# Two expert tables gathered apart in rows of 4 KB, the second by four tokens' 32 picks, on one Trainium2 core

## What is computed

```python
def block(args):
    xt, it, gt = args                     # tokens, 128 picks, 128 gates
    act = jax.nn.gelu(jnp.einsum('td,tkd->tk', xt, peer_u[it]), approximate=False)
    return jnp.einsum('tk,tkd->td', gt * act, peer_v[it])
```

## Time and profile before

| | us |
|---|---|
| median of three runs | 2607.96 |
| the runs | 2607.25 to 2612.75 |
| span of the profiled execution | 2607.3 |
| PE busy | 2152.8 |
| DVE busy | 1647.3 |
| ACT busy | 1003.4 |
| POOL busy | 702.4 |

### The profile page before, as it was taken

One profiled execution on the slowest core, in us unless ns is written; L12 is line 12 of the kernel. 1 busy time (PEld: TensorE's weight loads), 2 busy tenths in 40 slices (PEclk: granted clock), 3 DMA queues, 4 the chain that ended last, 5 costly groups with the idle time before them and its releaser, 6 DMA issues. The chain is left out here.

```text
span 2607.3 us, 25567 instructions
## 1 busy us (share of the span) xinstructions
PE 2152.8 (83%) x8090; PEld 1334.7 (51%) x8090; DVE 1647.3 (63%) x3381; ACT 1003.4 (38%) x2477; POOL 702.4 (27%) x610
## 2 busy tenths in 40 slices
PE   6999978897878687877868887676777787899998
PEld 6778855676423232322324453232333474788877
DVE  5674266535888988878456776656766555555534
ACT  3213345323443343333334344435533455433322
POOL 0120031000444354443434454444444100000000
PEclk8999988998999899898989999787988897999999
DMA  7664200211899999999999999999999433222222
GB/s 243 218 208 113 67 5 26 77 61 75 340 419 420 400 403 420 396 420 398 415 380 415 414 414 411 420 370 359 420 419 420 159 92 122 91 97 97 80 81 97
DMA packets 142827, 683.18 MB, mean 262 GB/s; under 512 B 19648, under 2 KB 36320, under 8 KB 74224
## 3 DMA queue, kind: packets, MB, share of 16 engines
q0 software_dynamic: 73728, 536.90, 50.3%
q1 hardware_dynamic: 68976, 144.78, 17.0%
HBM read 679.50 MB, written 2.10 MB: 261 GB/s over the span
## 5 line engine op out<-in xcount | busy, mean ns | idle before, releaser
L2483 PE MATMUL peer_Y<-peer_w,peer_diag 128*128 128x512 f32 x1784 | 902.5, 645 | 242.2 <-ACT peer_diag L2469 215.2
L2428 POOL DMA_INDIRECT peer_w<-in_peer_uv,peer_eidx x510 | 606.4, 1189 | 703.7 <-PE peer_Y L2483 465.8
L2437 DVE CUSTOM_DVE_ANT_0 peer_w<-peer_w,peer_xtok 128x1024 f32<-128x1024 f32 x510 | 617.7, 1222 | 198.1 <-DMA peer_w<-in_peer_uv,peer_eidx 195.3
L2483 PEld LDWEIGHTS peer_Y<-peer_w,peer_diag 128*128 128x128 f32 x1784 | 337.8, 202 | 753.2 <-ACT peer_diag L2469 443.7
L2461 ACT ACTIVATE peer_gel<-peer_dots 128x1 f32<-128x1 f32 x512 | 103.8, 203 | 721.8 <-DVE peer_dots L2437 721.5
L2469 ACT ACTIVATE peer_diag<-all_ident,peer_a 128x128 f32<-128x128 f32 x448 | 179.8, 401 | 18.1 <-PE peer_Y L2483 3.6
L2463 ACT ACTIVATE peer_a<-peer_gel,peer_gates 128x1 f32<-128x1 f32 x512 | 150.8, 294 | 16.6
L2992 PE MATMUL m_acc<-m2x_hs,m2x_cut 128*128 128x512 f32 (+1 forms) x384 | 143.7, 374 | 6.4 <-PEq L123 3.7
L2993 PE MATMUL m_acc<-m2x_hs,m2x_cut 128*128 128x512 f32 (+1 forms) x384 | 143.3, 373 | 0.0
L2994 PE MATMUL m_acc<-m2x_hs,m2x_cut 128*128 128x512 f32 (+1 forms) x384 | 143.2, 373 | 0.0
L1293 ACT ACTIVATE p_cut<-m1h_raw 128x512 fp32r<-128x512 f32 (+2 forms) x96 | 58.2, 609 | 202.1 <-PE p_acc L1240 119.3
(11 more groups left out here) (518 smaller groups left out, 3731.2 us busy)
## 6 DMA issues: line engine op xcount, KB each, us to landing
m_gates<-in_w_ada SPq DMA_DIRECT2D x48, 512.0 KB, 4.3
m2x_raw<-in_w_up SPq DMA_DIRECT2D x22, 1024.0 KB, 4.8
m1h_raw<-in_w_in SPq DMA_DIRECT2D x80, 256.0 KB, 3.1
m20h_raw<-in_w_in SPq DMA_DIRECT2D x48, 256.0 KB, 7.3
m22h_raw<-in_w_in SPq DMA_DIRECT2D x48, 256.0 KB, 2.8
m_down_ring<-in_w_down SPq DMA_DIRECT2D x22, 512.0 KB, 3.4
m_out_ring<-in_w_out SPq DMA_DIRECT2D x16, 512.0 KB, 7.8
peer_w<-in_peer_uv,peer_eidx POOLq DMA_INDIRECT x510, 16.7
```

The source lines that it names most:

```text
L2428: pool.indirect_dma_start(self.slot(n).rearrange("p c n -> p (c n)"), None, self.uv_dram, bass.IndirectOffsetOnAxis(self.col(self.eidx, n) ...
L2437: dve.tensor_tensor_reduce(u, u, self.xtok[:, n // PICKS, :], 1.0, 0.0, ALU.mult, ALU.add, self.col(self.dots, n)).then_inc(self.dotted, 1)
L2483: ins = pe.matmul(self.Y[:, h, :], self.diag[:, i % self.RD, :], self.slot(n)[:, 1, h * BANK:(h + 1) * BANK], start=(k == 0), stop=(i == l ...
```

## The change

- The two tables stay apart in memory. One indirect DMA fetches 128 rows of 4 KB from one of them: 512 DMAs for `u`, 512 for `v`. The ring has 16 slots of 512 KB and 4 lent ones.
- The order of the fetches is `u` 0 to 31 alone, then `u` s and `v` s - 32 in turn, then the last 32 of `v` alone. A step of the gather now ends 33 steps after its `u`: `STANDALONE` is 289, `STEPS` 545.
- A `u` fetch takes one pick of 128 tokens, as before. A `v` fetch takes 32 picks of four tokens: partition 32i + r holds pick r of token 4b + i of the tile. For this, tokens are dealt to partitions (token 4b + i at partition 32i + b): by 16 more DMAs from `xtok` to `xrow` in `norm_rows`, issued on SP behind the early loads, SP waiting for them, and by a permuted copy of the queries into `qT`. The picks and the weights are transposed in blocks of 32 x 32 by DVE: `eidxT` (one more piece in each top-k call), `aT`.
- ACT makes gelu for 32 picks at once, DVE the gated weights, ACT places them in `Z`, which holds for each of 32 fetches 128 x 32 stationary values, zero outside of the token's own picks. DVE clears `Z` once ahead of the first step.
- PE sums over the 128 partitions of a `v` fetch: output of 32 tokens, on column strip q of the array for fetches 8q + m. Four fetches make a batch, eight matmuls of 32 stationary columns and 512 moving ones, and the batch frees its four slots at its end. There are no diagonals, and none of the picks is folded on DVE.
- DVE takes two pieces of the top-k a step in the first 32 steps, three up to step 112, then two.

The core of the diff:

```diff
-    RW, RD = 9, 4
-    LOW, FIRST = 2, 4
-    FOLDED = range(2 * PICKS, NT * PICKS)
-    SHARE = 4
+    RW = 16
+    LOW, FIRST = 4, 8
+    GROUP = 32
+    GROUPS = NT * PICKS // GROUP
+    BATCH = 4
...
+        for s in range(self.N + self.GROUP):
+            if s < self.N:
+                self.order.append(("u", s))
+            if s >= self.GROUP:
+                self.order.append(("v", s - self.GROUP))
...
+    def consumed(self, item):
+
+        kind, n = item
+        return (self.dotted, n + 1) if kind == "u" else (self.used, n // self.BATCH + 1)
...
     def fetch(self, pool, limit):
         for n in range(self.fetched, limit):
+            kind, i = self.order[n]
             if n == self.FIRST:
                 pool.wait_ge(*self.vacated)
-            if n % (2 * TOPK) == 0:
-                pool.wait_ge(self.picked, TopK.picked_at(n))
+            if i % self.GROUP == 0:
+                pool.wait_ge(self.picked if kind == "u" else self.idx_turned, TopK.picked_at(i))
             if n >= self.RW + len(self.lent):
-                pool.wait_ge(*self.consumed(n - self.RW))
-            pool.indirect_dma_start(self.slot(n).rearrange("p c n -> p (c n)"), None, self.uv_dram,
-                                    bass.IndirectOffsetOnAxis(self.col(self.eidx, n), 0)).then_inc(self.landing(n)[0], 16)
+                pool.wait_ge(*self.consumed(self.order[n - self.RW]))
+            t, k = divmod(i, PICKS)
+            if kind == "u":
+                table, idx = self.u_dram, self.eidx[:, t, k:k + 1]
+            else:
+                b = self.token_row(i)
+                table, idx = self.v_dram, self.eidxT[:, t, k // self.GROUP * self.GROUP + b:k // self.GROUP * self.GROUP + b + 1]
+            pool.indirect_dma_start(self.slot((kind, i)), None, table, bass.IndirectOffsetOnAxis(idx, 0)).then_inc(self.landing((kind, i))[0], 16)
...
+        if s < self.N:
+            dve.wait_ge(*self.landing(("u", s)))
+            u = self.slot(("u", s))
+            dots = self.dots[:, s // self.GROUP % 2, s % self.GROUP:s % self.GROUP + 1]
+            dve.tensor_tensor_reduce(u, u, self.xrow[:, s // PICKS, :], 1.0, 0.0, ALU.mult, ALU.add, dots).then_inc(self.dotted, 1)
...
+            dve.tensor_tensor(self.a[:], self.gel[:], self.gates[:, t, k:k + self.GROUP], ALU.mult).then_inc(self.weighed, 1)
+            dve.wait_ge(self.weighed, g + 1)
+            if g >= 1:
+                dve.wait_ge(self.placed, 4 * g)
+            dve.transpose(self.aT[:], self.a[:]).then_inc(self.turned, 1)
...
+            for i in range(4):
+                rows = slice(32 * i, 32 * i + 32)
+                dst = self.Z[rows, g % 2, :].rearrange("p (q x) -> p q x", q=4)[:, :, i:i + 253:36]
+                act.activation(dst, self.aT[rows, :].rearrange("p (q r) -> p q r", q=4), ACT.Copy).then_inc(self.placed, 1)
...
+        for item in items:
+            pe.wait_ge(*self.landing(item))
         for h in range(2):
-            ins = pe.matmul(self.Y[:, h, :], self.diag[:, i % self.RD, :], self.slot(n)[:, 1, h * BANK:(h + 1) * BANK],
-                            start=(k == 0), stop=(i == last))
+            for q, item in enumerate(items):
+                b = self.token_row(item[1])
+                ins = pe.matmul(self.Y[32 * q:32 * q + 32, h, :], self.Z[:, g % 2, 32 * b:32 * b + 32], self.slot(item)[:, h * BANK:(h + 1) * BANK],
+                                start=(first % PICKS == 0), stop=(first % PICKS == PICKS - self.BATCH))
         ins.then_inc(self.used, 1)
...
-    FAST, PACES = 112, (3, 2)
-    done_by = lambda s: PACES[0] * min(s + 1, FAST) + PACES[1] * max(0, s + 1 - FAST)
+    SLOW, FAST = 32, 112
+    done_by = lambda s: 2 * (s + 1) + max(0, min(s + 1, FAST) - SLOW)
...
+            dve.memset(gather.Z[:], 0.0).then_inc(gather.zeroed, 1)
...
             load_early(sp, early_landed, early)
+            if dealt is not None:
+                for t in range(NT):
+                    sp.wait_ge(scaled, t + 1)
+                    for i in range(4):
+                        sp.dma_start(dealt[32 * i:32 * i + 32, t, :], xn[i:P:4, t, :]).then_inc(dealt_out, 16)
+                sp.wait_ge(dealt_out, 16 * 4 * NT)
...
+            dve.wait_ge(self.picked, call + 1)
+            dve.transpose(self.eidxT[:, t, ks], self.eidx[:, t, ks]).then_inc(self.turned, 1)
```

More of the change, by code:

```diff
@@ L2278, in vector @@
         hs, ks = slice(h0, h0 + n), slice(h0 * K, (h0 + n) * K)
-        stage = max(j for j in range(22) if self.start(call, j) <= i)
+        stage = max(j for j in range(23) if self.start(call, j) <= i)
         j = i - self.start(call, stage)
@@ L2452, in vector @@
+        t, at = divmod(s - self.GROUP, PICKS)
+        if at == 0 and t >= 1:
+            dve.wait_ge(self.used, t * PICKS // self.BATCH)
             for h in range(2):
@@ L2471, in tensor @@
     def tensor(self, pe, s):
-        n = s - 1
-        if not 0 <= n < self.N or not self.on_pe(n):
+        first = s - self.GROUP - self.BATCH + 1
+        if first < 0 or first % self.BATCH or first >= self.N:
             return
-        t, k = divmod(n, PICKS)
-        i = self.products(n)
-        pe.wait_ge(self.diaged, i + 1)
-        pe.wait_ge(*self.landing(n))
-        if k == 0 and t >= 1:
+        g, m = divmod(first // self.BATCH, self.GROUP // self.BATCH)
+        t = first // PICKS
@@ L2485, in tensor, with pick @@
         ins.then_inc(self.used, 1)
-def pick(nc, gather, top, qT, keys, mod, rows, steps):
-    ident = gather.consts["ident"]
-    FAST, PACES = 112, (3, 2)
-    done_by = lambda s: PACES[0] * min(s + 1, FAST) + PACES[1] * max(0, s + 1 - FAST)
+def pick(nc, gather, ident, top, qT, keys, mod, rows, steps):
+    SLOW, FAST = 32, 112
+    done_by = lambda s: 2 * (s + 1) + max(0, min(s + 1, FAST) - SLOW)
     calls = range(1, len(TopK.CALLS))
@@ L2557, in _ @@
         def _(pool):
-            gather.fetch_to(pool, gather.STEPS + 3)
+            gather.fetch_to(pool, gather.STEPS)
         @block.vector
```

144 lines of the change are left out of this document (71 added, 73 removed).

## The result

The changed kernel takes 2835.9 us, the median of four runs (2830.3 to 2845.6), where the kernel before took 2607.6 beside it (2606.8 to 2612.8). The ratio is 1.0878, with a 95% interval of 1.0854 to 1.0902: slower by 228 us, against 180 forecast. Where a text says first or second measurement, it means these two.

What follows compares the result with a forecast made beforehand. Transfers bounded the gather before; POOL's issues were to bound it after the change. The span of 2607.3 us plus 10 for dealing x and 170 for the longer gather gave 2787, forecast as 2788 us, range 2635 to 2890.

Steps and rivals of the forecast that it cites:

- Bound and sign: In the gather, POOL replaces the DMA engines as bound: 2.98 us per pair against 2.5 of transfer; slower, chance 0.92.
- An issue costs by rows: On POOL, an indirect DMA with its pause stays at 1.49 us for 128 rows, though the rows shrink to 4 KB.
- The price of a collision: On POOL, a dot product blocks an issue's start with chance 0.86, costing 0.53 us in the mean, 0.46 per dot.
- rival 2: In the gather, fixed dot timing hits each pair, or strips in turn make POOL wait for slots: 2935 us; chance 0.10.
- POOL waits for nothing: In the gather, POOL issues without waits for slots; its other work in the stretch adds only 11 us.
- The first 32 steps: At the gather's start, DVE paces steps at 2.0 us, 64 us in all; 44 issues begun by 734.4; memset 1.1.
- The deal of x: Before the query opens, SP's 16 uncovered DMAs take 7.0 us of issues and 2 to 3 to land: +10 us.
- Tail: Behind the gather's last issue, landing 3.4, last batch on PE 4 and two additions 1.3: +9 us.
- Behind the gather: After the last addition of Y, the remaining 571 us are untouched by the change.
- The four strips: On PE, a batch takes 8.1 us in turn, a quarter together; neither bounds; slot reuse needs 11.5 of 13.4 us.
- Rival 1: In the gather, transfers stay the bound: 2606 to 2665 us, 2640 at its middle; chance 0.22 for 2613 to 2700.
- Rival 3: In the gather, twenty half slots fill the transfer holes: 2566 us; chance 0.08 together with the lower edge of Rival 1.

Runs made afterwards that it cites:

- second measurement: The changed kernel, unchanged, measured again beside later experiments: 2785.4 us, ratio 1.0676.
- half rows: The changed kernel with rows of 2 KB, the fetched half of each used twice, so as many issues and half the bytes: 2857.8 us.
- first measurement: The changed kernel, unchanged, as first measured against the kernel before: 2835.9 us, ratio 1.0878.
- one-operand kernels: The changed kernel with dot products replaced by sums of the fetched row alone: 2691.9 us; with three norms' roots also made reciprocals on VectorE: 2655.2 us.

## Why the prediction came out as it did

The direction, the mechanism and nearly the size were right: 2788 forecast, 2836 and 2785 measured. That the second lies 3 us from the forecast is luck: two terms of the sum are off by over 60 us each, in opposite directions. Its steps one by one.

*Bound and sign.* POOL takes the place of the transfers. Right: the rate fell to 354 to 375 GB/s, POOL's waits for slots from 466 to 48 us, and halving the bytes gained nothing. POOL's busy time in the stretch was to be about 1230 us; it is 1171 (1024 x 1.134 and 10 of roots).

*An issue costs by rows.* Right, and the choice that carries the forecast: 1.13 us for rows of 4 KB where 1.19 had been taken over from 8 KB; undisturbed 0.95 for both, and for 2 KB no less. One of the supports of 1.49 was misread: from the issue at 669.06 to that at 680.79 there are seven steps and not eight, 1.68 us each and not 1.47, so this stretch did not agree with the mean. The sum rests on the mean alone.

*The price of a collision.* Mis-sized. I took a chance of 0.86 at 0.53 us, 0.46 for a dot. In the second measurement 475 of 512 dots are met by a start, 0.93, but such an issue takes 1.26, only 0.31 over 0.95. Starts are not spread evenly over a dot but locked to it, a fixed time behind the landing; rival 2 had named that as a risk, and here the phase falls kindly. With half rows it falls badly, 0.48. An issue with its pause came to 1.42, not 1.49: 980 x 0.07 = 69 us less than the sum has (1.43 in the first measurement, 59 less).

*POOL waits for nothing.* The step that failed. I gave POOL's other work +11 and found no wait in its way; in the second measurement the pauses over 0.35 us are 73 in all, in the first 108. I had looked for who is held up when DMAs are moved past a queue, but only on SP; the roots on POOL itself are behind twice as many issues, and their reader is VectorE, which frees the slots. The reciprocal in their place takes 45 us off. In the second measurement this error and the last nearly cancel, +62 and −69; in the first they don't, +97 and −59, and that is most of the 48 us by which it missed the forecast.

*The first 32 steps.* They were to take 64 us, with other than 64 as a sign of being wrong in the small; they took 60 (first dot product 681.12, that of step 32 at 740.91, first measurement). That 44 issues had begun by 744.4 (734.4 and 10), the 44th at 743.2, is then in part luck: the eleven steps up to it, from the 33rd issue at 724.48, took 1.70 us each where I took 1.49. The memset took 1.76 where I took 1.1.

*The deal of x.* +10: the first fetch came 9.7 us later in the first profile, but 17.8 later in the second (679.4 against 661.6), and 12 to 17 in the six variants that leave the deal where it was. The edit that covers the deal opens the gather some 7 earlier. The time gained by it, 5 us, is within the intervals. So this term was priced low for most executions.

*Tail.* +9 behind the last issue; it was 15.2 in the first measurement and 13.2 in the second; landing and last batch were priced too low. *Behind the gather* 571 was unchanged, as taken.

*The four strips.* Left open between in turn (8.1 us a batch) and together. The row of a batch in the kernel after, at the lower clock:

```profile
1006.85 3.64 PE L2520 MATMUL peer_Y<-peer_w,peer_Z 128*32 128x512 f32 x16 [7.46 <-DMA peer_w<-in_peer_v,peer_eidxT]
```

Sixteen records in 3.6 us at 1.2 GHz, and another batch (at 1667.35) in 1.92 at 2.4: four strips run together, and the slot condition of the prediction never came near.

*The rivals.* Rival 1, transfers as the bound, is what the one-operand kernels show: 2655 to 2692, inside its band once issues cost 0.97. Rival 3 needed an issue with its pause under 1.25; even the one-operand kernels have 0.97 + 0.30 = 1.27, and 4 KB rows came to 410 GB/s at best there. Rival 2's lock between a dot product and its row's issue is there, but at a phase that costs less than the mean.

## What to carry to other kernels

Before splitting a gather, price the issue, not the bytes: here 1 us of POOL to spare per DMA became a deficit of 0.3 us per pair, and halving the row doubles the bill. When a queue loses its slack, list everything else that stands in it and who reads that: a 1.7 us root behind fourteen fetches stopped the engine that frees the slots; taking such roots off the queue gave back some 45 us, and asking for them three units earlier perhaps 19. And measure such a kernel more than once: this one showed 50 us between two measurements where the kernel before showed 0.3.

## What the chip showed that was not expected

An issue on GpSimd that starts during a VectorE instruction with two SBUF operands ends some 0.8 us behind it (2969 of 2969 beside a dot product; 1.26 to 1.43 us in the mean for a start during one). It is not stretched by a sum of the same length with one operand (0 of 732), nor by a copy from PSUM into SBUF (0 of 9), but it is by a one-operand scaling that takes 0.75 us for 1024 elements (1.48). Rows of 4 KB reach 405 to 410 GB/s at full DMA share, rows of 8 KB 420. Four column strips of 32 run their fp32 matmuls together, 16 records in 3.64 us and at the higher clock in 1.92. And a DMA share of 0.96 to 0.99 went with 354 to 375 GB/s while POOL was the bound: here the share didn't tell how much bandwidth was used.
